# A two-layer hybrid decoder step: small loads by need, state-space rounds over two banks at once, and small tiles moved behind the down projection

## The reference

```python
D_MODEL, SEQ, DEPTH, DEC_BATCH, PAGE_SIZE = 1024, 256, 2, 8, 128
D_FF, CONV_W, PLE_DIM, SSM_WIDTH, SSM_STATE = 2816, 3, 256, 512, 64
def rmsnorm(x, g):
    y = xf * lax.rsqrt(jnp.mean(xf * xf, axis=-1, keepdims=True) + EPS)
    return (y * g.astype(jnp.float32)).astype(x.dtype)
# per layer, h is the residual stream:
#   xn = RMSNorm(h); one projection xn @ w_in gives queries, three kinds of k and v,
#        branch gates, the S5 input u (512 wide) and two merge gates
#   A  = sparse attention (compressed, selected and window branch) @ w_a
#   B  = S5: 32 groups, each a 64-dim complex diagonal state, associative scan over
#        positions, y = Re(C s) + D u, GELU, GLU
#   h += (sigmoid(gA) * A + sigmoid(gB) * B) @ w_o
#   [gate | value] = RMSNorm(h) @ w_up; gate -> causal conv (width 3) -> GELU
#   h += (GELU(conv) * value) @ w_down
#   h += sigmoid(RMSNorm(h) @ w_ple_gate) * (p[i] @ w_ple)
```

## Time and profile before

| what | value |
| --- | --- |
| median of 3 runs | 1222.62 us (1215.73 to 1223.17) |
| the profiled execution | 1222.28 us |
| its span, first to last instruction | 1220.6 us |
| PE busy in the span | 1138.2 us (93%), 6314 matmuls |
| DVE, ACT, POOL busy | 476.2, 282.3, 161.7 us |
| mean granted TensorE clock | 0.975 |

### The profile page before, as it was taken

One profiled execution on the slowest core, in us unless ns is written; L12 is line 12 of the kernel. 1 busy time (PEld: TensorE's weight loads), 2 busy tenths in 40 slices (PEclk: granted clock), 3 DMA queues, 4 the chain that ended last, 5 costly groups with the idle time before them and its releaser, 6 DMA issues.

```text
span 1220.6 us, 16573 instructions
## 1 busy us (share of the span) xinstructions
PE 1138.2 (93%) x6314; PEld 932.2 (76%) x6314; DVE 476.2 (39%) x1267; ACT 282.3 (23%) x885; POOL 161.7 (13%) x360
## 2 busy tenths in 40 slices
PE   4799998989999999999999799988999999999995
PEld 2677776668888888888778677756888888888874
DVE  3487743543233222243343876254223223220032
ACT  2333422430021111110224242244002111110021
POOL 5335330000300000002301725000000000000000
PEclk9899998899999999999999999899999999999998
DMA  9543473124655555344545338421444555435530
GB/s 228 154 114 98 126 263 74 51 70 146 152 147 154 138 145 144 99 143 129 190 118 174 103 111 260 116 74 55 154 121 138 139 160 150 127 107 155 149 105 35
DMA packets 239424, 162.24 MB, mean 133 GB/s; under 512 B 25344, under 2 KB 233240, under 8 KB 239208
## 3 DMA queue, kind: packets, MB, share of 16 engines
q1 hardware_dynamic: 229858, 144.45, 40.9%
q0 software_dynamic: 4752, 14.58, 4.2%
q10 hardware_dynamic: 4736, 2.16, 0.7%
HBM read 157.94 MB, written 7.58 MB: 136 GB/s over the span
## 4 chain that ended last, share of the span: by engine, by line
PE 83%; DVE 10%; SPq 2%; issue 2%; ACT 1%; DMA 1%; POOL 0%; DVEq 0%; POOLq 0%; ACTq 0%
PE bank_act L680 38%; PE bank_dve L680 35%; DVE kT L1710 2%; PE bank_dve L981 1%; SPq L426 1%; PE bank_act L1047 1%; DVE vpast L1702 1%; DVE Sf L1715 1%; PE bank_o L1010 1%; DVE Sf L1703 1%; PE bank_o L1061 1%; DMA PT<-in_cache_sel_dram 1%; DVE vpast L1706 0%; PE bank_act L856 0%; DVE pcw L1720 0%
## 5 line engine op out<-in xcount | busy, mean ns | idle before, releaser
L680 PE MATMUL bank_act<-xn,ring 128*128 128x264 f32 x1600 | 379.3, 395 | 0.5 <-ACT pcw L1182 0.5
L680 PEld LDWEIGHTS bank_act<-xn,ring 128*128 128x128 f32 x1600 | 309.7, 195 | 60.1 <-issue 4.8
L680 PE MATMUL bank_dve<-xn,ring 128*128 128x264 f32 x704 | 163.8, 386 | 0.0
L680 PE MATMUL bank_dve<-R,ring 128*128 128x264 f32 x704 | 157.6, 386 | 0.0
L680 PEld LDWEIGHTS bank_dve<-xn,ring 128*128 128x128 f32 x704 | 133.8, 190 | 22.9
L680 PEld LDWEIGHTS bank_dve<-R,ring 128*128 128x128 f32 x704 | 133.4, 190 | 22.6
L1891 DVE TENSOR_SCALAR PT<-GX,PT 128x264 f32<-128x264 f32 x44 | 18.4, 417 | 217.0 <-ACT GX L1182 212.1
L1182 ACT ACTIVATE GX<-bank_act 128x264 f32<-128x264 f32 x44 | 17.2, 391 | 270.8 <-PE bank_act L680 270.8
L628 POOL DMA_DIRECT2D out_dram<-kall x2 | 1.0, 519 | 474.7 <-ACT kall L1182 474.7
L1182 ACT ACTIVATE xn<-hT 128x264 f32<-128x264 f32 x32 | 13.5, 423 | 208.0 <-DVE hT L1908 149.8
L680 PE MATMUL bank_act<-ring,xn 128*128 128x256 f32 (+1 forms) x256 | 60.4, 389 | 0.0
(11 more groups left out here) (359 smaller groups left out, 1394.7 us busy)
## 6 DMA issues: line engine op xcount, KB each, us to landing
ring<-in_w_up_dram SPq DMA_DIRECT2D x88, 512.0 KB, 5.0
ring<-in_w_in_dram SPq DMA_DIRECT2D x28, 1024.0 KB, 5.6
ring<-in_w_down_dram SPq DMA_DIRECT2D x32, 704.0 KB, 4.6
ring<-in_w_glu_dram SPq DMA_DIRECT2D x16, 512.0 KB, 4.3
ring<-in_w_o_dram SPq DMA_DIRECT2D x8, 1024.0 KB, 5.0
ring<-in_w_ple_gate_dram SPq DMA_DIRECT2D x8, 1024.0 KB, 5.2
PT<-in_cache_cmp_dram SPq DMA_DIRECT2D x64, 64.0 KB, 2.6
ring<-in_w_a_dram SPq DMA_DIRECT2D x8, 512.0 KB, 6.2
```

The source lines that it names most:

```text
L680: ins = pe.matmul(out, lhsT, rhs, start=(k == 0), stop=(k == nk - 1))
```

## The change

There are five parts.

1. **Start.** SP's 16 small loads become 7 early ones (bias, ones, three masks, eye, page table: early_in) before chunk 1 and 9 later ones before chunk 3. PE, ACT, POOL and SP's page loads wait for early_in; DVE and PE wait for the others behind the S5 rounds and in attention. The transposes of the parameters move behind two of the eight x tiles, and DVE makes the angles after its copies of hT.
2. **Page tiles.** cache_rows stands LAG jobs later (3 in layer 0, 1 in layer 1), and STEPS_AT, OUTPUTS_AT and PAGES_AT get new numbers; the loop runs past the 15 jobs by LAG and one page more.
3. **S5 rounds.** The three bank_dve banks become one tensor, so DVE reads both banks of a round in one operation, and adds the sample states straight into HH. The two copies of states (hs, hfin) move from DVE to ACT, behind its share of outputs(q). A table is made by six operations of 256 elements, from rot0 and a second small table rot8.
4. **First up tile.** Its gate half and value half take rows with the gain only (gained(L, 1, o), made on DVE behind each w_o tile), sum_squares(1) stands behind its gate half, and conv(0) and gated(0) scale by rstd. The transposes of the convolution state and the PLE input move between the w_o tiles.
5. **PLE tiles.** All eight stand behind the down projection, with sum_squares(2) after the second.

```diff
-CONSTS = 16
+CONSTS, EARLY = 9, 7
...
-STEPS_AT = ((4, 5, 6, 7, 8, 10, 11, 12), (3, 4, 5, 6, 7, 9, 10, 11))
-OUTPUTS_AT = ((6, 7, 8, 9, 11, 12, 13, 14), (5, 6, 7, 8, 10, 11, 12, 13))
+LAG = (3, 1)
+STEPS_AT = ((4, 6, 7, 8, 9, 10, 11, 12), (3, 4, 5, 6, 7, 8, 9, 10))
+OUTPUTS_AT = ((7, 8, 9, 10, 11, 12, 13, 15), (5, 6, 7, 8, 9, 10, 11, 12))
...
-PAGES_AT = {5: (2,), 8: (3,), 9: (4, 5), 11: (6,), 12: (7,)}
+PAGES_AT = ({8: (2,), 9: (3,), 11: (4, 5), 12: (6, 7)}, {8: (2, 3), 9: (4,), 11: (5, 6), 12: (7,)})
...
-                    if L == 0 and m == 1:
+                    if L == 0 and m in (1, 3):
...
-                            sp.wait_ge(consts_in, 16 * CONSTS)
+                            sp.wait_ge(early_in, 16 * EARLY)
...
-                params_turned(0, dve_bank)
                 pe.wait_ge(x_in, 32)
                 for k in range(KD):
+                    if k == 2:
+                        params_turned(0, dve_bank)
...
-                        for k in range(4):
-                            n = 1 << k
-                            link(turn(rot0[:, :, :, 0:n], k + 1, 0, ST, n, [rot0[:, c, :, n:2 * n] for c in range(2)]))
+                        for table, first, steps in ((rot0, 1, 4), (rot8, 5, 3)):
+                            for k in range(steps):
+                                n = 1 << k
+                                link(turn(table[:, :, :, 0:n], first + k, 0, ST, n, [table[:, c, :, n:2 * n] for c in range(2)]))
...
-                        T = rot[:, q % 2]
...
+                        pool.tensor_tensor(T[0], near[0], far[0], ALU.mult)
+                        pool.tensor_tensor(w[0], near[1], far[1], ALU.mult)
+                        pool.tensor_tensor(T[1], near[0], far[1], ALU.mult)
+                        link(pool.tensor_tensor(w[1], near[1], far[0], ALU.mult))
+                        pool.tensor_tensor(T[0], T[0], w[0], ALU.subtract)
+                        pool.tensor_tensor(T[1], T[1], w[1], ALU.add).then_inc(rot_ready, 1)
...
-                        cache_rows(jobs)
...
+                    if jobs >= LAG[L]:
+                        cache_rows(jobs - LAG[L])
...
-                    for j in range(2):
-                        i = 2 * q + j
...
-                        tt(W1[:, j], bu[:, :, 0:HALF], co, MUL)
-                        tt(W2[:, j], bu[:, :, 0:HALF], si, MUL)
-                        tt(new_s[:, i], bu[:, :, HALF:UW], old_s[:, i], ADD).then_inc(dve_freed, 1)
...
+                    tt(W1, bu[:, :, :, 0:HALF], co, MUL)
+                    tt(W2, bu[:, :, :, 0:HALF], si, MUL)
+                    h = HH[:, q % 2]
+                    if q >= 2:
+                        dve.wait_ge(y_ready, L * NQ + q - 1)
+                        dve.wait_ge(states_taken, L * NQ + q - 1)
+                    tt(h[:, :, :, HALF:UW], bu[:, :, :, HALF:UW], old_s[:, 2 * q:2 * q + 2], ADD).then_inc(dve_freed, 2)
...
-                    dve.tensor_copy(h[:, :, :, HALF:UW], new_s[:, 2 * q:2 * q + 2])
-                    dve.tensor_copy(hfin[:].rearrange("p c i -> p i c")[:, 2 * q:2 * q + 2], h[:, :, :, HALF - 1]).then_inc(state_ready, 1)
...
+                    fn(hfin[:].rearrange("p c i -> p i c")[:, 2 * q:2 * q + 2], h[:, :, :, HALF - 1]).then_inc(states_taken, 1)
...
-                sum_squares(1)
-                pe.wait_ge(act_freed, act_jobs(L, "ple_in", 2))
-                columns(512, 4, pT, 2, act_bank, act_ready)
...
                             if f == 0 and half == 0:
+                                pe.wait_ge(hg_ready, (2 * L + 1) * KD + k + 1)
+                            if f == 1 and half == 0:
                                 normed_to(1, k)
-                            last = mm(bank[:, 0:NT], w[:, k, P * half:P * half + P], xn[:, k, :], k, KD)
+                            last = mm(bank[:, 0:NT], w[:, k, P * half:P * half + P], hgT[k] if f == 0 else xn[:, k, :], k, KD)
                         last.then_inc(ready, 1)
+                        if f == 0 and half == 0:
+                            sum_squares(1)
...
+                    if f == 0:
+                        link(tt(tg[:, 0, :], tg[:, 0, :], rstd[:], MUL))
```

More of the change, by code:

```diff
@@ L1147, in layer @@
                             direct(L + 1, dve_bank)
-                sum_squares(2)
+                w = next_chunk()[:, 0:2 * 512].rearrange("p (k n) -> p k n", k=2)
+                pe.wait_ge(act_freed, act_jobs(L, "ple_in", 2))
+                for j in range(4):
+                    bank = act_bank()
+                    for k in range(2):
+                        last = mm(bank[:, 0:NT], w[:, k, P * j:P * j + P], pT[:, k, :], k, 2)
+                    last.then_inc(act_ready, 1)
+                    if j == 1:
+                        sum_squares(2)
                 columns(512, 4, pT, 2, act_bank, act_ready)
@@ L1318, in inputs @@
                         last.then_inc(act_freed, 1)
-                jobs = 0
-                for c0, w in QW_CHUNKS:
-                    for t in range(3):
+                for jobs in range(2 * NB + LAG[L]):
+                    if jobs < JOBS:
+                        t = jobs % 3
+                        c0, w = QW_CHUNKS[jobs // 3]
                         bank = take(base)
```

233 lines of the change are left out of this document (133 added, 100 removed).

## The result

The changed kernel takes 1189.05 us (median of 4 runs, 1188.44 to 1194.63) against 1222.89 us (4 runs, 1215.73 to 1224.04): a ratio of 0.9745, with a 95% interval of 0.9698 to 0.9793. The profiled execution took 1188.44 us, with a span of 1186.8. The prediction was 1192 us, range 1181 to 1204. That the total is so near is in part luck: the terms that were forecast sum to 26.1 us in the trace, and 7.7 us come from stretches that no term named.

A forecast was written before the change was run, and what follows sets the result against it. PE was taken to carry the span, with DVE's rounds the bound where PE arrives early. Terms -15.6, -0.8, -3.7, -4.8 and -5.0 sum to -29.9: from 1222.28 to 1192.4, stated as 1192 us, range 1181 to 1204.

The forecast's parts named there:

- Start: First instruction to layer 0's u tiles: job 0 starts at 16.5, u tiles at 31.4 against 47.04, -15.6 us.
- Clock in job 0: First weights' matmuls at the start: job 0 stays at half clock and lasts 6.28 us, as before.
- the fourth rival: More gain: job 0 at full clock (-2.7) or the last page pair in time (-8.2); 1181 to 1190, chance 0.19.
- Rounds: S5 rounds on DVE: a round falls from 7.63 to about 6.3 us, with scans at 1.65 instead of 2.46.
- Layer 0's stretch: Layer 0's u tiles and rounds: -5.8 gap, -4.6 clock, +1.4 page tiles, +6.2 wait, +2 clock; -0.8 us.
- The page wait: End of layer 0's rounds: PE waits 6.2 us for the last pair of pages, whose trip takes 8.3.
- The clock's 4.6: Layer 0's u tiles and rounds: the 4.6 us lost to the lowered clock goes with the gaps.
- Layer 1's rounds: Layer 1's u tiles and rounds: -7.5 gap, -1.8 clock, +0.45 page tile, +2.5 DVE waits, +1.5 page wait; -4.8 us.
- The page wait of 1.5: Layer 1's rounds: a wait for pages with LAG 1, kept in the sum at +1.5 us.
- Layer 1's start and the feed-forward layers: Layer 1's start -3.7 us; first up tile and PLE tiles in the feed-forward layers -2.5 per layer, -5.0 both.
- The first rival: S5 rounds stay near 7.6 us, the two round stages give some 4 us less each: 1200, chance 0.14.
- The slower rival: SP's queue: page pairs wait for ACT ahead of weight chunks, PE loses 30 us; above 1222, chance 0.02.

The follow-up runs named there:

- fillers: Changed kernel with spare matmuls where TensorE waits, ahead of layer 0's u tiles and in both layers' attention: 1187.13 us.
- LAG 2: Changed kernel with page tiles two jobs late instead of three in layer 0: 1190.50 us, ratio 0.9752 to the kernel before.
- the run with the old order: Changed kernel with the feed-forward layer as before (normalised rows for the first up tile, four PLE tiles ahead of it, transposes behind w_o): 1200.34 us.

## Why the prediction was right, and where it was right for the wrong reason

The length of attention of layer 0, unchanged work of 938 matmuls, over the kernels: 171.31 before, 164.92 after, and with the experiments in the order above 170.52, 165.10, 165.67, 170.75, (165.24 with fillers), 168.87, 171.14, 164.92, 171.11, 171.02, and 162.51 and 164.65 with fillers. These lengths don't follow what was altered. PE's idle time in the stretch is 12.6 us in every kernel without spare matmuls, so all of the difference is busy time on the same work, and the slices show the clock as its cause. That it depends on the moment at which a stretch begins is the reading that fits. The varying job 0 speaks for it, but no run shifts the time and nothing else, so it isn't shown. It isn't the chance of one execution either: the mean clock of the kernel before was 0.973 to 0.979 in 24 of its 25 executions beside the experiments (0.984 in the other), and that of the changed kernel 0.989 in three of four. So 6.4 + 1.3 us of the measured 33.8 are the clock's, and the parts that the prediction summed are worth 26.1 against its 29.9. No term of the prediction failed badly, but a term was missing: it let unchanged stretches keep their time.

- **Start**, -15.6 forecast, -16.0 measured. The place and the chain of numbers held: job 0 at 16.2, half clock, u tiles at 31.0. But the first half of x is there at 6.5 (my 10.0 came from a median over both halves), and chunk 0 at 3.2 + 7.7 = 10.9, not at 19.1, because GpSimd's loads waited. I had put that wait at nothing, neither cost nor gain, and had the page table's place as what held job 0. By the runs it is the other way round: 5.5 us for GpSimd's wait, 0.5 at most for the tables. The other 10 us (the x tiles ahead of the parameters, the page tile and its wait gone from behind job 0) are read from the rows and were tested by no run.
- **Clock in job 0**, 6.28 forecast, 6.1 measured. Full clock in job 0, the first half of the fourth rival, did not come. The Trainium skill's "TensorE: Matmul & The Clock Gate", Part 1, says that activity releases the clock; that the transposes directly ahead would do was the rival's own step, and the changed kernel shows that they don't. Spare matmuls did it. That 6.1 is so near is partly luck, since job 0 varied by 1.4 us over kernels with the same start.
- **Rounds**. The step that failed is "a round becomes about 6.3 us": it is 7.2. The scans gained nearly what was said (1.78, forecast 1.65); but what GpSimd slowed moved to two additions, which the sum left as they were and which became 0.73 us longer together. The old tables give the same round, so the shorter table work was worth nothing. The table itself was put at 3.9 us and takes 4.6 (645.09 to 649.66).
- **Layer 0's stretch**, -0.8 forecast, +1.3 measured. Three sizes were off and partly made up for each other. The gap on DVE did not vanish, it fell from 5.8 to 3.3 (L832 and L821 in this stretch). The page wait was 2.6 + 0.3, not 6.2: the tile that comes first needs only the key pages, which are there 5.8 us after ACT's copy (its end at 115.60, the tile at 121.44) and not 8.3, and PE spent 1.9 of that waiting for the last round. The clock's 4.6 did not come back: two new waits, ahead of the u tiles and at the last pages, cost it again (0.95 as before). The spare matmuls gave 1.7 us of this back at the first, and LAG 2 gave 3.85, with the wait, at the second.
- **Layer 1's rounds**, -4.8 and -3.0: the same 7.2 us a round; of the waits on DVE 5.2 us are left, where I kept 2.5. The page wait of 1.5 that I kept did not come, which made up for part of it.
- **Layer 1's start and the feed-forward layers**: -3.7, and -2.3 and -2.4 against -2.5 each, as reckoned, and the run with the old order returned 2.3 twice.

The first rival (the rounds stay long) came true by half: GpSimd's longer operations did take back most of the round's gain, but by way of the additions and not of the scans, which fell to 1.78. It cost some 4 us over both layers, where that rival had 8; the range held it. The slower rival did not show: the only page pair that PE waits for is the last.

## What to carry to other kernels

Cut two traces at the same instructions and look first at the stretches that the change leaves alone: here they moved by 7.7 us of 33.8, and in one run they hid a gain of 7.1 whole. A queue that only feeds later work can hold back the first weights: make such loads wait for the first ones that PE needs. Shortening what runs on a neighbouring engine need not spare the critical one: here GpSimd's time beside the rounds fell from 36.07 to 29.86 us and a round stayed as long. Without that work beside it the round was 1.35 us shorter, so look for a place where nobody waits. And fill PE's own waits where the clock falls behind them: here a fall behind a wait of 2.6 us cost 1.7 more.

## What the runs showed of the hardware that I had not expected

- The same 256-column addition on DVE takes 0.42 us alone and 0.84 to 0.95 beside GpSimd's 256-element operations, the scans 1.37 against 1.78 (or 2.33 beside the shorter ones). A round costs 5.86 us without GpSimd and 7.2 with it, in both ways of cutting its work, although one keeps GpSimd busy a fifth longer.
- GpSimd's 16 small loads, issued at the start, moved the landing of a 1 MB chunk on another queue from 7.7 to 16.0 us after its issue, and the issue of the page table on that queue from 7.45 to 14.94.
- An unchanged stretch of 938 matmuls took 164.9 to 171.3 us, by the granted clock alone. With matmuls without use in its waits it took 162.5 to 165.2 in three profiles; but layer 1's took 167.3 in one of these, so they don't rule it out.
- Behind a wait of 2.5 to 4.4 us ahead of the u tiles the granted clock of the next 6 us was 0.72 to 0.76 in ten profiles of ten; with that wait filled it was 1.00 in three of three.
